# Routing moved into the experts' stage: early loads of the first weights, bf16 products for prefix sums and token lists, products of constants in TensorE's holes

## The chip, the cores and the metric

The kernel runs on one core of one Trainium2 chip. The metric is the device time of one execution, in microseconds. Three runs of the kernel before took 1526.89, 1527.82 and 1534.71 us, a median of 1527.82.

## What is computed

The program is one decoder layer over 1024 tokens of width 1024 in float32: an input projection, two groups of attention heads, an output projection, then a mixture of experts, then a gated per-layer embedding and a last normalisation. The change touches the head of the mixture of experts:

```
grp_logits = u @ w_group + b_group;  g_star = argmax(grp_logits)
in_prob = softmax(the 4 expert logits of g_star);  top_v, top_i = top_k(in_prob, 2)
w = grp_prob[g_star] * top_v / sum(top_v);  expert_id = g_star * 4 + top_i
for e in range(16):
    hid = silu(u @ w_gate_e[e]) * (u @ w_up_e[e])
    y += combine[e] * (hid @ w_down_e[e])
```

Each token goes to 2 of 16 experts. The kernel doesn't compute all 16 for every token. It sorts the 2048 (token, expert) pairs by expert into tiles of 128 rows, an expert's rows starting on a new tile, and computes tile by tile.

## The kernel before

The program is a row of stages. Each stage is a scope with its own semaphores, and a scope ends with a barrier of all engines, the clearing of its semaphores and a second barrier (`Scope.__exit__`, line 165). Within a stage every engine has a program of its own, written out by hand in the order in which it runs, and the engines meet at semaphores. The stages here are `stage_mix`, which ends with the routing logits in `lg`, then `stage_route`, then `stage_moe`, then `stage_finish`.

`stage_route` (scope `rte`) is one chain of small VectorE steps (L1676 to L1759), in which every step waits for the one before it. The maxima and the choices give `pick` (which expert for each of a token's two places) and `both` (their sum). Two float32 products on TensorE follow: `ps_r` (L1771), with a strictly triangular matrix, counts the earlier tokens of a block of 128 that chose the same expert, and `ps_t` (L1772), with a matrix of ones, gives each block's count. Eight additions over the blocks (L1707) give the prefix sums `off`. From the totals come the number of tiles of each expert, `cend` and `cbeg`, then `where` and the place `slot` of each pair. Then the list is turned round, from slot to token: `is_tile` (tile one-hot times token number) and `is_row` (row one-hot, 128x2048) are made on VectorE, and 16 float32 products sum them in `ps_s` (L1776). VectorE meanwhile makes the tile plan (`texp`, `last`, `tnew`, `tord`) and at last copies the list to `stok` (L1759).

`stage_moe` loops over the tiles. GpSimd copies a column of `stok` to `idx` (L1919) and gathers 128 rows of u with an indirect DMA into `xg` (L1921). TensorE turns them (L2106). ScalarE and VectorE split the result into a high and a low part (`xT_hi` L1964, `xT_lo` L2051). The sync engine (SP) loads an expert's weights in 8 chunks of gate and up (16 transfers at L1863) and 4 chunks of down (L1870). ScalarE and VectorE split each chunk as well (`g_hi` L1940, `g_lo` L2028). TensorE then does three products for each of 8 chunks and 2 matrices, 48 in all (`gate_up`, L138 to L140), turns the hidden values (L2124) and does 24 products for `down`. Each engine begins by reading `last` into a register (L1851). A chunk of the next expert's weights is loaded once both parts of the chunk before it are split. That wait stands in SP's program, so the chunks follow one another in order.

In `stage_moe` before the change, SP's program begins with the reads of `last` and of `texp` and then the 16 transfers for the first expert; ScalarE's begins with `x_part(0)`, then eight `split_g`; VectorE's with a memset of zeros, then `x_part(0)` and eight `split_g`.

Of the kernel before, what the change touches and what calls it, by code (L numbers as in the profile page):

```python
# [27 lines left out]
F32 = mybir.dt.float32  # L28
F32R = mybir.dt.float32r
BF16 = mybir.dt.bfloat16  # L30
I32 = mybir.dt.int32
# [1585 lines left out]
def stage_route(nc, K, T):  # L1617


    with Scope(nc, "rte") as sc:  # L1620
        def sb(name, *shape):
            return sc.sb(name, [P, *shape])

        gmax, gsum, gp, pm = (sb(n, NT) for n in ("gmax", "gsum", "gp", "pm"))
        dlt, pri, ohg, il, oh1, oh2, il2 = (sb(n, NT, 4) for n in ("dlt", "pri", "ohg", "il", "oh1", "oh2", "il2"))
        m1, m2, e2, v1 = (sb(n, NT) for n in ("m1", "m2", "e2", "v1"))
        prod = sb("prod", NT, NG, EPG)
        pick = [sb(f"pick{k}", NT, NG, EPG) for k in range(2)]
        both = sb("both", NT * NE)
        off = sb("off", NT + 1, NE)  # L1630
        tot = sb("tot", NT, NE)
        where = sb("where", NT, NE)
        cnt_i = sc.sb("cnt_i", [P, NE], I32)
        ntl, cend, cbeg, ones = (sb(n, NE) for n in ("ntl", "cend", "cbeg", "ones"))
        tile_ge = sb("tile_ge", 32, NE)
        tile_e = sb("tile_e", 32)
        tile_new = sb("tile_new", 32)
        tile_ord = sb("tile_ord", 32)
        n_last = sb("n_last", 1)
        slot_f = sb("slot_f", 2, NT)  # L1640
        row_f = sb("row_f", 2, NT)
        in_tile = sb("in_tile", 2, NT)
        slot_i = sc.sb("slot_i", [P, 2, NT], I32)
        is_row = sb("is_row", 2 * NT, P)
        is_tile = sb("is_tile", 2 * NT, SLOTS // P)
        ps_r = sc.ps("ps_r", [P, 512])
        ps_t = sc.ps("ps_t", [P, 512])
        ps_s = sc.ps("ps_s", [P, 512])
        own_dve, expd, want_exp, ranked, both_made, slots_made, named = (
            sc.sem(n) for n in ("own_dve", "expd", "want_exp", "ranked", "both_made", "slots_made", "named"))  # L1650
        c = K["c"]
        lg = K["lg"]
        with sc.block() as block:
            @block.vector
            def _(dve):
                own = Tally(own_dve)

                def step(ins):
                    own.inc(ins)
                    own.wait(dve)  # L1660

                V = nc.vector

                def wide(x, n=4):

                    return x[:].unsqueeze(2).to_broadcast((P, NT, n))

                def first_max(x, top, out):

                    step(V.tensor_tensor(pri[:], x, wide(top), ALU.is_equal))  # L1670
                    step(V.tensor_tensor(pri[:], pri[:], c[:, K_PRI:K_PRI + 4].unsqueeze(1).to_broadcast((P, NT, 4)),
                                         ALU.mult))
                    step(V.tensor_reduce(pm[:], pri[:], X, ALU.max))
                    step(V.tensor_tensor(out[:], pri[:], wide(pm), ALU.is_equal))

                step(V.memset(ones[:], 1.0))  # L1676
                step(V.tensor_reduce(gmax[:], lg[:, :, 0:NG], X, ALU.max))
                V.tensor_tensor(dlt[:], lg[:, :, 0:NG], wide(gmax), ALU.subtract).then_inc(want_exp, 1)
                first_max(lg[:, :, 0:NG], gmax, ohg)
                step(V.tensor_tensor(prod[:], lg[:, :, NG:].rearrange("p t (g j) -> p t g j", g=NG),  # L1680
                                     ohg[:].unsqueeze(3).to_broadcast((P, NT, NG, EPG)), ALU.mult))
                step(V.tensor_reduce(il[:], prod[:].rearrange("p t g j -> p t j g"), X, ALU.add))
                step(V.tensor_reduce(m1[:], il[:], X, ALU.max))
                first_max(il[:], m1, oh1)
                step(V.scalar_tensor_tensor(il2[:], oh1[:], NEG, il[:], ALU.mult, ALU.add))
                step(V.tensor_reduce(m2[:], il2[:], X, ALU.max))
                first_max(il2[:], m2, oh2)
                V.tensor_tensor(e2[:], m2[:], m1[:], ALU.subtract).then_inc(want_exp, 1)
                for k, oh in enumerate((oh1, oh2)):
                    step(V.tensor_tensor(pick[k][:], ohg[:].unsqueeze(3).to_broadcast((P, NT, NG, EPG)),  # L1690
                                         oh[:].unsqueeze(2).to_broadcast((P, NT, NG, EPG)), ALU.mult))
                V.tensor_tensor(both[:], pick[0][:].rearrange("p t g j -> p (t g j)"),
                                pick[1][:].rearrange("p t g j -> p (t g j)"), ALU.add).then_inc(both_made, 1)

                dve.wait_ge(expd, 2)
# [10 lines left out]
                for t in range(NT):  # L1706
                    step(V.tensor_tensor(off[:, t + 1, :], off[:, t, :], tot[:, t, :], ALU.add))  # L1707
# [761 lines left out]
```

## Time and profile before

| | us |
|---|---|
| median of three runs | 1527.82 |
| the profiled execution's own time | 1527.78 |
| its span | 1525.8 |
| TensorE busy in the span | 1370.0 (90%) |
| VectorE busy | 759.3 (50%) |
| ScalarE busy | 628.8 (41%) |
| GpSimd busy | 166.6 (11%) |

The span runs from the first to the last instruction, and the execution's own time is 2.0 us longer. All positions below are in us from the start of the span. The last logits are copied at 898.04, routing's own chain lasts from 900.60 to 925.27, and the products of the first tile begin at 941.23. The granted TensorE clock is given as a share of full speed: 1.00 is 2.4 GHz and 0.50 is 1.2 GHz.

### The profile page before, as it was taken

Reading aid. Unit: us, or ns where it says so; the run is one execution under the profiler, and the core shown is the slowest. Engines: PE = TensorE matmul, PEld = TensorE weight load, DVE = VectorE, ACT = ScalarE, POOL = GpSimd, SP = SyncE. Lnnn points to the kernel's source line nnn. Section 1 sums busy time; section 2 is a strip of 40 time slices with the busy share of each in tenths; the row PEclk is TensorE's granted clock in tenths of the full one; section 3 lists DMA queues with packets and bytes.
Section 4 is the critical chain, followed back from the end, with each engine's and each line's share of the span. In section 5 each row is a group of like instructions: output and inputs, shape, how many; then the busy total and the mean of one; then the engine's idle time right before and its main releaser. Section 6 shows DMA issues by size and latency. Waiting matters only on the chain. (4 is left out here: it accounts for less than half of the span.)

```text
span 1525.8 us, 24075 instructions
## 1 busy us (share of the span) xinstructions
PE 1370.0 (90%) x7956; PEld 1157.9 (76%) x7957; DVE 759.3 (50%) x1225; ACT 628.8 (41%) x932; POOL 166.6 (11%) x164
## 2 busy tenths in 40 slices
PE   5899999959999999999789955999999999928996
PEld 4788879949989988888678844777777787716774
DVE  4734013344544444433353344678655767846562
ACT  5312121023333334454442212567645666743442
POOL 2100000041111122322000000000100000011000
PEclk9999999969999999999889966999999999968998
DMA  7333311051100111443132206799976979784411
GB/s 249 96 89 110 117 60 52 3 125 26 26 22 22 36 43 43 126 112 71 39 117 97 110 28 237 274 324 382 353 247 234 351 291 350 275 313 138 135 61 42
DMA packets 107556, 222.23 MB, mean 146 GB/s; under 512 B 14717, under 2 KB 41389, under 8 KB 107478
## 3 DMA queue, kind: packets, MB, share of 16 engines
q1 hardware_dynamic: 95462, 178.87, 35.7%
q0 software_dynamic: 8608, 30.51, 5.7%
q10 hardware_dynamic: 3408, 11.80, 2.1%
q8 instruction: 50, 0.82, 0.2%
q14 instruction: 28, 0.23, 0.0%
HBM read 176.56 MB, written 36.24 MB: 139 GB/s over the span
## 5 line engine op out<-in xcount | busy, mean ns | idle before, releaser
L1253 ACT ACTIVATE att_prob<-att_ps_s 128x512 f32<-128x512 f32 (+1 forms) x240 | 134.6, 561 | 246.5 <-PE att_ps_s L1180 201.6
L1302 DVE TENSOR_REDUCE att_mx<-att_ps_m 128x1 f32<-128x512 f32 (+3 forms) x256 | 132.8, 561 | 134.5 <-PE att_ps_m L1127 122.8
L2028 DVE TENSOR_TENSOR exp_g_lo<-exp_g_raw,exp_g_hi 128x1024 fp32r<-128x1024 f32 x128 | 148.1, 1220 | 43.3 <-ACT exp_g_hi L1940 43.3
L138 PE MATMUL moe_ps_g<-exp_g_hi,moe_xT_hi 128*128 128x512 f32 x336 | 137.7, 410 | 16.8 <-DVE exp_g_lo L2028 16.8
L1940 ACT ACTIVATE exp_g_hi<-exp_g_raw 128x1024 fp32r<-128x1024 f32 x128 | 124.8, 1047 | 40.7 <-PE moe_ps_g L140 25.5
L1198 PE MATMUL att_ps_o<-tok_vsw,att_prob 128*128 128x65 f32 x1056 | 140.1, 274 | 0.0
L139 PE MATMUL moe_ps_g<-exp_g_lo,moe_xT_hi 128*128 128x512 f32 x336 | 133.9, 399 | 0.0
L140 PE MATMUL moe_ps_g<-exp_g_hi,moe_xT_lo 128*128 128x512 f32 x336 | 133.9, 398 | 0.0
L1198 PEld LDWEIGHTS att_ps_o<-tok_vsw,att_prob 128*128 128x128 f32 x1056 | 131.2, 192 | 2.6 <-ACT att_prob L1253 0.5
L138 PE MATMUL prj_ps_w<-prj_hT_hi,prj_w_hi 128*128 128x512 f32 x256 | 102.3, 399 | 5.6 <-ACT prj_w_hi L425 2.4
L140 PE MATMUL prj_ps_w<-prj_hT_hi,prj_w_lo 128*128 128x512 f32 x256 | 101.3, 396 | 0.0
L139 PE MATMUL prj_ps_w<-prj_hT_lo,prj_w_hi 128*128 128x512 f32 x256 | 101.3, 396 | 0.0
L138 PEld LDWEIGHTS moe_ps_g<-exp_g_hi,moe_xT_hi 128*128 128x128 f32 x336 | 64.0, 191 | 37.5 <-DVE exp_g_lo L2028 20.2
L2033 DVE TENSOR_TENSOR exp_d_lo<-exp_d_raw,exp_d_hi 128x1024 fp32r<-128x1024 f32 x64 | 74.0, 1220 | 21.8 <-ACT exp_d_hi L1946 21.8
L138 PE MATMUL moe_ps_y<-exp_d_hi,moe_hT_hi 128*128 128x512 f32 x168 | 68.9, 410 | 10.8 <-DVE exp_d_lo L2033 10.8
L1198 PE MATMUL att_ps_o<-tok_vb,att_prob 128*128 128x65 f32 x576 | 75.9, 273 | 0.0
L140 PEld LDWEIGHTS moe_ps_g<-exp_g_hi,moe_xT_lo 128*128 128x128 f32 x336 | 63.8, 190 | 15.6
L139 PEld LDWEIGHTS moe_ps_g<-exp_g_lo,moe_xT_hi 128*128 128x128 f32 x336 | 64.2, 191 | 13.8
L1198 PEld LDWEIGHTS att_ps_o<-tok_vb,att_prob 128*128 128x128 f32 x576 | 72.1, 192 | 1.9 <-ACT att_prob L1253 0.2
L1919 POOL COPY moe_idx<-all_stok 128x1 uint32 (+1 forms) x22 | 10.2, 463 | 551.3 <-PE moe_ps_x L2106 339.5
L1946 ACT ACTIVATE exp_d_hi<-exp_d_raw 128x1024 fp32r<-128x1024 f32 x64 | 62.3, 1045 | 19.1 <-issue 19.1
L433 ACT ACTIVATE att_w_out<-prj_ps_w 128x512 f32<-128x512 f32 x28 | 16.7, 598 | 124.3 <-PE prj_ps_w L140 124.3
(357 smaller groups left out, 2950.2 us busy)
## 6 DMA issues: line engine op xcount, KB each, us to landing
exp_g_raw<-in_w_gate_e SPq DMA_DIRECT2D x128, 256.0 KB, 4.7
exp_g_raw<-in_w_up_e SPq DMA_DIRECT2D x128, 256.0 KB, 5.4
exp_d_raw<-in_w_down_e SPq DMA_DIRECT2D x64, 512.0 KB
y_rows<-moe_y ACTq DMA_DIRECT2D x21, 512.0 KB, 6.1
prj_w_raw<-in_w_in SPq DMA_DIRECT2D x16, 512.0 KB, 4.0
att_q_raw<-feat SPq DMA_DIRECT2D x32, 256.0 KB, 4.9
feat<-att_w_out POOLq DMA_DIRECT2D x14, 512.0 KB, 2.9
att_k_raw<-feat SPq DMA_DIRECT2D x24, 256.0 KB, 6.0
```

The source lines that it names most:

```text
L138: nc.tensor.matmul(out, a_hi, b_hi, start=first, stop=False)
L139: nc.tensor.matmul(out, a_hi, b_lo, start=False, stop=False)
L140: return nc.tensor.matmul(out, a_lo, b_hi, start=False, stop=last)
L433: nc.scalar.activation(feat[:, s, h * 512:(h + 1) * 512], ps_w[:, h, :], ACT.Copy, scale=scale).then_inc(evac, 1)
L1198: last = nc.tensor.matmul(ps_o[:, u % 2, (q % 4) * HV:(q % 4 + 1) * HV], prob[:, b % PT, at + (q - qa) * P:at + (q - qa + 1) * P], value(k ...
L1253: nc.scalar.activation(prob[:, b % PT, 0:w], ps_s[:, b % ST, 0:w], ACT.Exp, scale=-1.0).then_inc(expd, 1)
L1302: last = nc.vector.tensor_reduce(mx[i % 2][:, col, q:q + 1], p[:, at:at + (kb - ka) * P], X, ALU.min)
L1919: nc.gpsimd.tensor_copy(idx[:], K["stok"][:, bass.ds(i, 1)]).then_inc(idx_set, 1)
L1940: nc.scalar.activation(g_hi[:, ch % GR], g_raw[:, ch], ACT.Copy).then_inc(s_ghi, 1)
L1946: nc.scalar.activation(d_hi[:, ch % DR], d_raw[:, ch], ACT.Copy).then_inc(s_dhi, 1)
L2028: nc.vector.tensor_tensor(g_lo[:, ch % GR], g_raw[:, ch], g_hi[:, ch % GR].bitcast(F32), ALU.subtract).then_inc(s_glo, 1)
L2033: nc.vector.tensor_tensor(d_lo[:, ch % DR], d_raw[:, ch], d_hi[:, ch % DR].bitcast(F32), ALU.subtract).then_inc(s_dlo, 1)
```

## The change

`stage_route` is gone as a stage. Its steps become the head of the engines' programs in `stage_moe`, without the barriers in between. Its tiles lie in the memory of the buffer `h`, which is filled much later, so they show as `exp_h`. Within the steps:

- The triangular matrix and the matrix of ones are cast to bf16 on GpSimd (`below`), and `both`, `is_row` and `is_tile` are bf16. The eight additions are replaced by eight bf16 products that add each block's counts to all later blocks and to a total in one PSUM tile.
- The first expert is named as soon as the totals are known (`e0`), and SP loads its 16 chunks behind that (`first_named`). The rest of the plan is signalled at the end (`planned`), and each engine reads `last` later.
- The token list is summed as two numbers (row in the block, block), each small enough for bf16. They are put together by one VectorE step, which signals `tokens_made` to GpSimd.
- ScalarE splits four chunks and VectorE two before they take the first x tile.
- TensorE runs 10, 16 and 20 products of constants (`spin`) before the counts, before the lists and before the first x tile. Their output is overwritten.

```diff
+def spin(nc, out, K, n):
+    for _ in range(n):
+        nc.tensor.matmul(out, K["c"][:, K_ID:K_ID + P].bitcast(BF16)[:, 0:P], K["c"][:, 0:2 * P].bitcast(BF16),
+                         start=True, stop=True)
...
             @block.sync
-                end = last_used(sp)
-                e0 = sp.value_load(K["texp"][0:1, 0:1], min_val=0, max_val=NE - 1)
-                load_g(e0)
+                sp.wait_ge(first_named, 1)
+                e0 = sp.value_load(K["e0"][0:1, 0:1], min_val=0, max_val=NE - 1)
+                load_g(e0)
+                sp.wait_ge(planned, 1)
+                end = last_used(sp)
...
             @block.gpsimd
-                end = last_used(pool)
+                nc.gpsimd.tensor_copy(below, c[:, K_LT:K_LT + 2 * P]).then_inc(ones_made, 1)
...
+                pool.wait_ge(tokens_made, 1)
                 gather(0)
+                pool.wait_ge(planned, 1)
+                end = last_used(pool)
...
             @block.scalar
-                end = last_used(act)
-                x_part(0)
-                for ch in range(GC):
-                    split_g(0, 0, ch, False)
+                for ch in range(EARLY):
+                    split_g(0, 0, ch, False)
+                x_part(0)
+                for ch in range(EARLY, GC):
+                    split_g(0, 0, ch, False)
+                act.wait_ge(planned, 1)
+                end = last_used(act)
...
             @block.vector
+                dve.wait_ge(ranked, 1)
+                step(V.tensor_scalar(ntl, ps_r[:, NT * NE:(NT + 1) * NE], float(P - 1), None, ALU.add))
...
+                step(V.tensor_scalar(none, cend, 0.5, None, ALU.is_lt))
+                step(V.tensor_reduce(e0_f[:, 0:1], none, X, ALU.add))
+                V.tensor_copy(K["e0"][:], e0_f[:, 0:1]).then_inc(first_named, 1)
...
+                step(V.scalar_tensor_tensor(where, cbeg.unsqueeze(1).to_broadcast((P, NT, NE)), float(P),
+                                            ps_r[:, 0:NT * NE].rearrange("p (t e) -> p t e", t=NT), ALU.mult, ALU.add))
...
+                step(V.tensor_scalar(is_tile[:, :, 0:32], hit.rearrange("p k t n -> p (k t) n"), c[:, K_TOK:K_TOK + 1], None,
+                                     ALU.mult))
...
+                V.scalar_tensor_tensor(K["stok"][:], found[:, 32:32 + SLOTS // P], float(P), found[:, 0:SLOTS // P],
+                                       ALU.mult, ALU.add).then_inc(tokens_made, 1)
...
             @block.tensor
-                end = last_used(pe)
+                spin(nc, ps_g[:, 0, :], K, 10)
+                pe.wait_ge(ones_made, 1)
+                pe.wait_ge(both_made, 1)
+                nc.tensor.matmul(ps_r[:, 0:NT * NE], below[:, 0:P], both, start=True, stop=False, skip_group_check=True)
+                for t in range(NT):
+                    n = NT - t
+                    last = nc.tensor.matmul(ps_r[:, (t + 1) * NE:(NT + 1) * NE], below[:, P:2 * P],
+                                            both[:, t * NE:(t + 1) * NE].unsqueeze(1).to_broadcast((P, n, NE)),
+                                            start=False, stop=t == NT - 1, skip_group_check=True)
+                last.then_inc(ranked, 1)
+                spin(nc, ps_g[:, 0, :], K, 16)
+                pe.wait_ge(slots_made, 1)
+                for n in range(2 * NT):
+                    last = nc.tensor.matmul(ps_s[:, 0:64], is_row[:, n, :], is_tile[:, n, :], start=n == 0,
+                                            stop=n == 2 * NT - 1)
+                last.then_inc(named, 1)
+                spin(nc, ps_g[:, 0, :], K, 20)
                 turn_x(0, True)
                 gate_up(0, True)
+                pe.wait_ge(planned, 1)
+                end = last_used(pe)
```

Three places show how rows move. On TensorE, between the end of the mixing stage and the first x tile, the difference of the two orders is this (L1620 is a product of constants, `exp_h` holds routing's tiles, L2106 turns the first x tile):

```order
-L1771 MATMUL rte_ps_r<-rte_both,all_c 128x128
-L1772 MATMUL rte_ps_t<-rte_both,all_c 128x128
-L1776 MATMUL rte_ps_s<-rte_is_tile,rte_is_row 128x32 x16
-L1653 UNCONDITIONAL_BRANCH
 L2095 UNCONDITIONAL_BRANCH
-L1851 TENSOR_LOAD all_last
-L1851 ISA x2
+L1620 MATMUL moe_ps_g<-all_c 128x512 x10
+L2143 MATMUL moe_ps_y<-exp_h 128x128
...
+L1620 MATMUL moe_ps_g<-all_c 128x512 x16
+L2153 MATMUL moe_ps_h<-exp_h 128x64 x16
+L1620 MATMUL moe_ps_g<-all_c 128x512 x20
```

One branch and the read of `last` are gone ahead of the first x tile, and 46 products of constants are new. On VectorE, before, from the token list to the first hidden tile:

```order
L1759 CAST all_stok<-rte_ps_s 128x32
L1653 UNCONDITIONAL_BRANCH
L2024 UNCONDITIONAL_BRANCH
L2066 MEMSET moe_zeros 128x256
L1851 TENSOR_LOAD all_last
L1851 ISA x2
L2051 TENSOR_TENSOR moe_xT_lo<-moe_ps_x,moe_xT_hi 128x512 x2
L2028 TENSOR_TENSOR exp_g_lo<-exp_g_raw,exp_g_hi 128x1024 x8
L2058 TENSOR_TENSOR moe_hid<-moe_act_g,moe_ps_g 128x512
```

And the same place on VectorE now, where the list (L2049) is followed by the rest of the plan up to `tord` (L2061):

```order
L2048 COPY exp_h<-moe_ps_h 128x64
L2049 SCALAR_TENSOR_TENSOR all_stok<-exp_h 128x32
...
L2061 CAST all_tord<-exp_h 128x32
L2062 MEMSET moe_zeros 128x256
L1923 TENSOR_TENSOR exp_g_lo<-exp_g_raw,exp_g_hi 128x1024 x2
L1946 TENSOR_TENSOR moe_xT_lo<-moe_ps_x,moe_xT_hi 128x512 x2
L1923 TENSOR_TENSOR exp_g_lo<-exp_g_raw,exp_g_hi 128x1024 x6
L1734 TENSOR_LOAD all_last
L1734 ISA x2
L1953 TENSOR_TENSOR moe_hid<-moe_act_g,moe_ps_g 128x512
```

The list is now made ahead of the plan, two of the eight weight splits stand ahead of the x tile's, and the stage's branches between them are gone.

## Rows read from the trace of the kernel before

**Rows 1.** Stretches: length, busy us (instructions) by engine, clock, DMA share, GB/s

```profile
926.00:936.00 10.00, 0.00 (x0) 0.00 (x0) 0.27 (x1) 0.00 (x0) 1.22 (x2) 0.50 0.65 217
1100.00:1300.00 200.00, 195.05 (x901) 156.86 (x900) 127.42 (x131) 118.13 (x140) 14.90 (x22) 1.00 0.81 291
```

**Rows 2.** Timeline, routing's first part: start, duration, engine, line, operation, [idle before]

```profile
898.04 0.33 DVE L1549 COPY all_lg<-mix_ps_l 128x160 f32<-128x160 f32 x1 [6.89 <-PE mix_ps_l L1600]
...
900.60 0.07 DVE L1676 MEMSET rte_ones<- 128x16 f32 x1 [2.23 <-PEq L165]
...
905.86 0.29 DVE L1692 TENSOR_TENSOR rte_both<-rte_pick 128x128 f32<-128x128 f32 x1
...
907.54 0.29 DVE L1704 COPY rte_tot<-rte_ps_t 128x128 f32<-128x128 f32 x1 [0.21 <-PE rte_ps_t L1772]
```

**Rows 3.** Timeline, VectorE from the prefix sums to the row one-hot

```profile
908.00 1.63 DVE L1707 TENSOR_TENSOR rte_off<-rte_off,rte_tot 128x16 f32<-128x16 f32 x8
909.67 0.17 DVE L1709 TENSOR_SCALAR rte_ntl<-rte_off 128x16 f32<-128x16 f32 x1
...
911.27 0.29 DVE L1718 SCALAR_TENSOR_TENSOR rte_where<-rte_cbeg,rte_where 128x128 f32<-128x128 f32 x1
...
915.58 2.29 DVE L1737 TENSOR_TENSOR rte_is_row<-all_c,rte_row_f 128x2048 f32<-128x2048 f32 x1
```

**Rows 4.** Timeline, the products of the token list and their copy

```profile
917.93 7.04 PE L1776 MATMUL rte_ps_s<-rte_is_tile,rte_is_row 128*128 128x32 f32 x32 [10.50 <-DVE rte_is_row L1737]
...
925.08 0.19 DVE L1759 CAST all_stok<-rte_ps_s 128x32 uint32<-128x32 f32 x1 [3.59 <-PE rte_ps_s L1776]
```

**Rows 5.** Timeline, from the list to the first tile's products

```profile
927.36 0.18 POOL L1919 COPY moe_idx<-all_stok 128x1 uint32<-128x1 uint32 x1 [211.81 <-issue]
928.09 0.36 SPq L1863 DMA_DIRECT2D exp_g_raw<-in_w_gate_e  x1
928.43 1.04 POOL L1921 DMA_INDIRECT moe_xg<-u_rows,moe_idx  x1 [0.89 <-POOL moe_idx L1919]
...
936.27 1.97 PE L2106 MATMUL moe_ps_x<-all_c,moe_xg 128*128 128x128 f32 x8 [11.31 <-DMA moe_xg<-u_rows,moe_idx]
...
937.42 0.39 SPq L1863 DMA_DIRECT2D exp_g_raw<-in_w_up_e  x1
...
939.85 9.18 DVE L2028 TENSOR_TENSOR exp_g_lo<-exp_g_raw,exp_g_hi 128x1024 fp32r<-128x1024 f32 x8 [0.25 <-ACT exp_g_hi L1940]
...
941.23 0.77 PE L138 MATMUL moe_ps_g<-exp_g_hi,moe_xT_hi 128*128 128x512 f32 x1 [2.98 <-DVE exp_g_lo L2028]
```

**Rows 6.** Timeline, TensorE: end of the first tile's 48 products, begin and end of another tile's

```profile
954.41 1.04 PE L2106 MATMUL moe_ps_x<-all_c,moe_xg 128*128 128x128 f32 x8
...
978.94 0.48 PE L138 MATMUL moe_ps_g<-exp_g_hi,moe_xT_hi 128*128 128x512 f32 x1
...
990.21 1.03 PE L2106 MATMUL moe_ps_x<-all_c,moe_xg 128*128 128x128 f32 x8
```

**Rows 7.** Stretches of the first tile's products, columns as in rows 1

```profile
942.00:945.00 3.00, 3.00 (x8) 2.32 (x8) 3.00 (x4) 3.00 (x4) 0.00 (x0) 0.50 1.04 395
947.00:954.00 7.00, 7.00 (x32) 5.63 (x31) 2.03 (x2) 0.75 (x1) 0.00 (x0) 1.00 1.05 387
```

**Rows 8.** The gathers of x: all 22, then the first alone

```profile
DMA to landing us min/median/max: 4.1/7.1/8.0
...
DMA to landing us min/median/max: 7.8/7.8/7.8
```

**Rows 9.** bf16 products (timeline); groups by form: busy, mean ns, idle before

```profile
401.06 0.39 PE L1127 MATMUL att_ps_m<-tok_maskb,tok_identb 128*128 128x128 bf16 x4
...
L558 DVE TENSOR_SCALAR att_sin<-att_sin,all_c 128x1024 f32<-128x1024 f32 x1 | 0.8, 755 | 1.2 <-ACT att_cos L463 1.2
...
L1029 POOL CAST att_w_two<-all_c 64x1024 fp32r<-64x1024 f32 x2 | 2.1, 1037 | 0.1
...
L1919 POOL COPY moe_idx<-all_stok 128x1 uint32 x21 | 10.0, 477 | 339.5 <-PE moe_ps_x L2106 339.5
```

More of the change, by code:

```diff
@@ L1827, in stage_moe, with small @@
         last_hi = sc.sem("last_hi")
+        (own_dve, expd, want_exp, ones_made, both_made, ranked, slots_made, named, first_named, planned, tokens_made) = (
+            sc.sem(n) for n in ("own_dve", "expd", "want_exp", "ones_made", "both_made", "ranked", "slots_made", "named",
+                                "first_named", "planned", "tokens_made"))
+        words = K["h"][:].rearrange("p a n -> p (a n)")
+        taken = 0
+        def small(*shape, dt=F32):
+            nonlocal taken
+            n = int(np.prod(shape)) // (2 if dt == BF16 else 1)
+            at, taken = taken, taken + n
+            v = words[:, at:taken]
+            if dt != F32:
+                v = v.bitcast(dt)
+            names = "abc"[:len(shape)]
+            return v if len(shape) == 1 else v.rearrange(f"p ({' '.join(names)}) -> p {' '.join(names)}",
+                                                         **dict(zip(names[1:], shape[1:])))
+        gmax, gsum, gp, pm, m1, m2, e2, v1 = (small(NT) for _ in range(8))
+        dlt, pri, ohg, il, oh1, oh2, il2 = (small(NT, 4) for _ in range(7))
+        prod = small(NT, NG, EPG)
+        pick = [small(NT, NG, EPG) for _ in range(2)]
+        where = small(NT, NE)
+        ntl, cend, cbeg, ones, none = (small(NE) for _ in range(5))
+        cnt_i = small(NE, dt=I32)
+        tile_ge = small(32, NE)
+        tile_e, tile_new, tile_ord = (small(32) for _ in range(3))
+        e0_f, n_last = small(2), small(2)
+        slot_f, row_f, in_tile = (small(2, NT) for _ in range(3))
+        slot_i = small(2, NT, dt=I32)
+        hit = small(2, NT, 32)
+        found = small(64)
+        both = small(NT * NE, dt=BF16)
+        below = small(2 * P, dt=BF16)
+        is_row = small(2 * NT, P, dt=BF16)
+        is_tile = small(2 * NT, 64, dt=BF16)
+        assert taken <= HB * D
+        lg = K["lg"]
+        ps_r, ps_s = ps_y[:, 0, :], ps_h[:]
         wl_d = a["w_ple_gate"].rearrange("l (k p) n -> (l k) p n", p=P)
@@ new lines, in _ @@
+                step(V.tensor_copy(tile_ge[:, :, 0], tile_new))
+                step(V.memset(tile_ge[:, :, 1], 1.0))
+                step(V.tensor_tensor_scan(tile_ord, tile_ge[:, :, 1], tile_ge[:, :, 0], 0.0, ALU.mult, ALU.add))
+                V.tensor_copy(K["tord"][:], tile_ord).then_inc(planned, 1)
+                nc.vector.memset(zeros[:], 0.0).then_inc(zero_made, 1)
+                for ch in range(2):
+                    split_g(0, ch)
+                x_part(0)
+                for ch in range(2, GC):
+                    split_g(0, ch)
@@ L2067, in _ @@
+                dve.wait_ge(planned, 1)
                 end = last_used(dve)
-                x_part(0)
-                for ch in range(GC):
-                    split_g(0, ch)
                 hidden(0)
@@ L2438, in build @@
             stage_mix(nc, a, K, T)
-        stage_route(nc, K, T)
         with Scope(nc, "exp") as exp:
```

218 lines of the change are left out of this document (78 added, 140 removed).

## The prediction

> **What bounds the kernel now.** I read the stretches first. While the experts run, TensorE is busy 195 of 200 us [rows 1], so a microsecond taken from before their first product should come off the end of the span as well, as long as the later tiles keep their distances. Then I read the timeline between the last logits at 898.04 [rows 2] and the first expert product at 941.23 [rows 5]. In these 43.2 us TensorE does little but wait. The chain is: barrier (2.2 us idle ahead of 900.60), VectorE's small steps up to the row one-hot at 915.58 [rows 2, 3], 16 list products (7.0 us) and the copy at 925.08 [rows 4], barrier to 927.36, gather issued at 928.43, x there at 936.27, x split, first weights split, product at 941.23 [rows 5]. Each is late only by the one before it. The weights' transfers begin at 928.09 and their last issue is at 937.42, beside the gather. In the ten microseconds 926 to 936 no compute engine but GpSimd and one memset works, and the clock stands at 0.50. The first 48 products take 13.18 us (941.23 to 954.41), those of a later tile 11.27 (978.94 to 990.21) [rows 5, 6], because the first ones find the clock at 0.50 and get 1.00 only on the way [rows 7].
>
> **The change part by part**, in positions of the trace of before.
>
> *Up to the counts.* The choices' steps are the same ones. The memset of ones moves from their front behind them, which evens out. `both` ends at about 906.1 as before. VectorE has six small steps for the weights of the combination to do and was only 0.21 us early at 907.54 [rows 2], so it is nearly ready whatever the counts cost. Four bf16 products fit in 0.39 us, pipeline latency included [rows 9], so nine take at most 0.9 us at full clock and 1.8 at half: counts at 907.1 to 908.0. I take 907.5, a gain of nothing (-0.1 to +0.5). The ten products of constants before them are 512 columns each like the experts', 11.27/48 = 0.235 us at full clock and at most twice that at half, 4.7 us. They start at 900.6 and are over by 905.3, before `both`.
>
> *Counts to row one-hot.* Gone: the copy of totals, the memset and the eight additions, 909.67 - 907.54 = 2.13 us [rows 2, 3]. A small step costs 1.67/8 = 0.21 us with its wait. New: compare, reduce and cast for `e0`, the cast without a wait, 0.5 us. Two steps for `where` become one, -0.33. The cast to `slot` moves behind, -0.21. The token number's product stays as two steps for the block, and a scalar product over 512 elements is added: 0.755 us for 1024 [rows 9] gives 0.38, with its wait 0.44. Sum: -2.13 + 0.5 - 0.33 - 0.21 + 0.44 = -1.73. `is_row` starts at 913.8 instead of 915.58 and its 2.35 us (915.58 to 917.93) stay, since its inputs are float32 as before and only the output is bf16. The lists start at 916.15.
>
> *The lists.* 32 float32 passes pairwise took 7.04 us at clock 0.50, 0.22 each [rows 4]. Now there are 16 bf16 products. At half clock each is at most a float32 record's half, 0.11, so 1.8 us, at full clock 0.9 to 1.6 by the 0.1 above. I take 2.0 with the end's latency: 918.15. VectorE's slot, tile comparison and reduction end at about 917.7, and do not hold it up. Two more steps (copy from PSUM, combination) 0.45: `tokens_made` at 918.6, against 925.27.
>
> *No barrier.* From there GpSimd's first copy stood 2.09 us later, at 927.36. A wait on a semaphore costs 0.2: 918.8. The gather is issued 1.07 later as before, at 919.9. That is 8.5 us early.
>
> *The weights.* `e0` comes after five small steps from the counts (four of 0.21 and a scan, 1.07) and the 0.5 above: 909.1. SP reads one register (two cost it 1.4 between 926.7 and 928.1, so 0.7) and starts at 909.9 instead of 928.09. 16 issues need 937.42 + 0.39 - 928.09 = 9.7 us, to 919.6, just before the gather. ScalarE then splits four chunks and VectorE two while x is on its way. VectorE has first to finish the plan, 2.4 us (the same steps as before), the zeros and two splits of 1.2, until 924. That is before x has come.
>
> *x arrives.* The first gather took 7.8 us in competition with the weights; the 22 lie between 4.1 and 8.0 [rows 8]. Now the weights' 4.2 MB, started 18 us earlier, are nearly all in when the gather starts. I take 5.8, between the two cases: 925.7 (bounds 924.0 and 927.9). TensorE's 20 products of constants run from 918.2 and take 4.7 us at full clock and at most 9.4 at half, ending 922.9 to 927.6. So they may hold x up by a microsecond: turning starts at 926.2, 10.1 us early.
>
> The Trainium skill, "Trainium Kernel Development and Optimization", Key Constraints, speaks against this place: transfers from the queues of SP, ScalarE and GpSimd all run on the same 16 DMA engines and interleave, so an early gather still shares them with the tail of the early weights. By that rule alone the landing stays near 7.8 us and the time is 2 us longer, still inside my range. The first gather's 7.8 against the least of 4.1 agrees with it.
>
> *x to first product.* Before: 936.27 to 941.23, of which x's own split ends at 939.60 (0.25 ahead of 939.85) and the rest is the first weights' split [rows 5]. That second part goes: 3.33 us remain, or 2.6 at full clock, where turning takes 1.04 [rows 6] instead of 1.97. I take 2.9: first product at 929.1, 12.1 us early. What is late next is x itself, no longer the weights. VectorE makes chunk 3's low part 1.2 us after x's, and TensorE asks for it 2.8 us after.
>
> *Clock.* The first 48 products cost 13.18 us when they start at half clock and 11.27 when at full. With 20 products of constants right before, I take 12.0, a gain of 1.2 (0 to 1.9).
>
> The Trainium skill, "TensorE: Matmul & The Clock Gate", Part 1, says that the array stands at half rate by default and that sustained work releases it. The fall to 0.50 before 941 and the return in rows 7 agree. By that rule the full 1.9 is had if constants run right up to x, none if the hole behind them is long.
>
> *What is unchanged.* The reads of `last` move behind work with slack: VectorE and ScalarE wait for TensorE at the first tile's end. From 954.41 on the order is the same and shifts as a whole.
>
> **Sum.** 12.1 + 1.2 = 13.3 us against the execution's own 1527.78, which is the median within 0.04: 1514.5. With the slowest landing, 3.33 and a cold start: 927.9 + 3.3 = 931.2, gain 10.0, less 0.5 for the counts, 1518.3. With the fastest landing, 2.6 and a warm start: 924.0 + 2.6 = 926.6, gain 14.6 + 1.9 = 16.5, so 1511.3.
>
> **Rivals.**
>
> *A. Late x, cold clock.* The gather is as slow as before or slower because the weights, not finished, share its engines, and the holes after the constants let the clock fall. For it: 7.8 us in the one case like it. Against: the issues are over when the gather starts. Gain 8 to 11, 1518.5.
>
> *B. The early steps don't run as written.* GpSimd's cast of two matrices to bf16, or VectorE's steps beside it, are slow. A cast of 64x1024 takes 1.04 us, so 256 columns 0.3 [rows 9], ready 5 us before it is needed. "GPSIMD Engine Reference" (the Trainium skill), its table's row on SBUF interfaces, says that GpSimd shares them with VectorE and that VectorE instructions with two SBUF inputs contend. The index copy agrees: 0.477 us among the weights' subtractions [rows 9], 0.18 alone [rows 5]. That would make 0.3 of the new gather's copy at most. It is slower than before only if the cast takes over 5.5 + 13.3 = 19 us from 900.6; every microsecond over 5.5 costs one, and a cast of 25 us would give 1534. Nothing in the rows comes near that.
>
> *C. The gain is given back.* The second expert's loads, or the tiles' later waits, don't move with the first product, because DMA at 395 GB/s [rows 7] is the bound there. Against: over the long stretch the DMA share is 0.81 and TensorE's 195 of 200 [rows 1], and loads start earlier than the products do. Gain under 7.6, say 1522.
>
> **Chances.** Forecast 0.65, A 0.25, C (and part of B) 0.08, B slower than before 0.02. The predicted time is the forecast's. The range 1510.5 to 1519.5 holds the sum's two ends and A, and leaves out C and B. A measurement of this kernel can tell 0.5%, 7.6 us, from no change: faster 0.92, same 0.06, slower 0.02.
>
> **What would show it.** In the new profile: first SP transfer of the experts 18 us ahead of before, list products under 2 us, GpSimd's first copy at about 918.8, 20 us or less after the first routing step, TensorE's first x tile at about 926, first product 2.6 to 3.3 us later, with a clock of 1.00 or soon. From the first tile's end to the span's end the distance should be 571.4 us as before (1525.8 - 954.4). I am wrong if that distance grows, if x lands later than 928, or if TensorE still works at the constants when x is there for more than 2 us.

## The result, and the profile after

The changed kernel takes 1518.27 us, the median of 7 runs (1516.01 to 1521.95). The kernel before, with runs beside these, has a median of 1529.42 of 7 (1526.89 to 1534.71). The ratio is 0.993 with a 95% interval of 0.9913 to 0.9947, so the change is 11 us faster (8 to 13). The forecast was 1514.5 in a range of 1510.5 to 1519.5, so the time came out inside the range and 3.8 us above the number. The profiled execution took 1516.79 us with a span of 1515.1, against 1527.78 and 1525.8 before.

The stages ahead of the change run a little earlier or later in each execution. So positions are counted here from the start of the copy of the last logits, which lies at 898.04 before [rows 2] and at 898.54 after. I write +30.5 for 30.5 us behind it. First the timeline of VectorE after (start, duration, engine, line, operation, idle before), answering to rows 2, 3 and 4:

```profile
898.54 0.32 DVE L1549 COPY all_lg<-mix_ps_l 128x160 f32<-128x160 f32 x1 [6.89 <-PE mix_ps_l L1600]
901.15 0.19 DVE L1980 TENSOR_REDUCE exp_h<-all_lg 128x8 f32<-128x32 f32 x1 [2.29 <-PEq L165]
...
907.76 0.17 DVE L2004 TENSOR_TENSOR all_cw<-all_cw,exp_h 128x8 f32<-128x8 f32 x1
907.97 0.17 DVE L2008 TENSOR_SCALAR exp_h<-moe_ps_y 128x16 f32<-128x16 f32 x1
...
914.32 2.29 DVE L2038 TENSOR_TENSOR exp_h<-all_c,exp_h 128x2048 bf16<-128x2048 f32 x1
...
917.46 0.69 DVE L2046 TENSOR_REDUCE exp_h<-exp_h 128x32 f32<-128x512 f32 x1
918.18 0.22 DVE L2048 COPY exp_h<-moe_ps_h 128x64 f32<-128x64 f32 x1
```

From behind 901.15 up to the list no row has idle time before it: in routing VectorE never waits for a product any more, neither for the counts (907.97, where it waited 0.21 before) nor for the lists (918.18, where it waited 3.59). Next TensorE after, with the products of constants (L1620) between the useful ones:

```profile
901.06 4.24 PE L1620 MATMUL moe_ps_g<-all_c 128*128 128x512 bf16 x10 [2.56 <-PEq L165]
906.75 0.22 PE L2143 MATMUL moe_ps_y<-exp_h 128*128 128x128 bf16 x1 [1.45 <-DVE exp_h L1995]
906.81 0.43 PE L2146 MATMUL moe_ps_y<-exp_h 128*128 128x128 bf16 x8
907.10 3.61 PE L1620 MATMUL moe_ps_g<-all_c 128*128 128x512 bf16 x16
916.67 1.03 PE L2153 MATMUL moe_ps_h<-exp_h 128*128 128x64 bf16 x16 [5.96 <-DVE exp_h L2038]
917.51 6.71 PE L1620 MATMUL moe_ps_g<-all_c 128*128 128x512 bf16 x20
926.35 1.10 PE L2106 MATMUL moe_ps_x<-all_c,moe_xg 128*128 128x128 f32 x8 [2.12 <-DMA moe_xg<-u_rows,moe_idx]
929.02 0.80 PE L138 MATMUL moe_ps_g<-exp_g_hi,moe_xT_hi 128*128 128x512 f32 x1 [1.57 <-DVE moe_xT_lo L1946]
...
941.78 1.04 PE L2106 MATMUL moe_ps_x<-all_c,moe_xg 128*128 128x128 f32 x8
```

The lists take 1.03 us instead of 7.04 [rows 4]. The first expert product now waits for x's low part (L1946), not for the weights' low part as in rows 5. It comes at +30.48, before at +43.19. GpSimd and SP after, answering to rows 5, and the first gather's landing, to rows 8:

```profile
918.70 0.18 POOL L1804 COPY moe_idx<-all_stok 128x1 uint32<-128x1 uint32 x1 [17.26 <-DVE all_stok L2049]
919.77 1.04 POOL L1806 DMA_INDIRECT moe_xg<-u_rows,moe_idx  x1 [0.90 <-POOL moe_idx L1804]
...
910.63 0.36 SPq L1746 DMA_DIRECT2D exp_g_raw<-in_w_gate_e  x1
...
DMA to landing us min/median/max: 6.5/6.5/6.5
```

And stretches of the kernel after (length, busy us of TensorE, its weight loads, VectorE, ScalarE, GpSimd, then clock, DMA share, GB/s), for rows 7:

```profile
907.00:911.00 4.00, 3.71 (x24) 1.55 (x21) 3.42 (x18) 0.00 (x0) 0.00 (x0) 1.00 0.01 2
911.00:916.00 5.00, 0.00 (x0) 0.00 (x0) 4.69 (x10) 1.06 (x1) 0.00 (x0) 0.92 0.79 279
916.00:922.00 6.00, 5.33 (x27) 2.45 (x28) 5.42 (x19) 3.17 (x3) 1.22 (x2) 0.50 1.05 390
922.00:928.00 6.00, 3.33 (x18) 1.64 (x16) 1.67 (x3) 0.95 (x2) 0.18 (x1) 1.00 0.83 288
929.00:932.00 3.00, 2.98 (x7) 2.43 (x8) 3.00 (x3) 2.98 (x5) 0.70 (x1) 0.50 0.52 143
```

The constants raise the clock to 1.00 twice, and it is lost again twice: during the hole of 5.96 us ahead of the lists, and at x. There it outlives the hole of 2.12 us, since turning still takes 1.10 us (1.97 at half clock, e2), and is gone behind the next one of 1.57 us. The first 48 products begin at 0.50, as before.

### The profile page after: what moved, and what is told of

Read it like the earlier page. It is cut to its first block and busy times, and to the rows that moved or that the text cites. A ratio compares the mean times of both kernels' runs of the same rounds, so it can differ in the third digit from the quotient of the medians.

```text
span 1515.1 us, 24106 instructions
## 1 busy us (share of the span) xinstructions
PE 1379.2 (91%) x7991; PEld 1158.4 (76%) x7992; DVE 758.6 (50%) x1219; ACT 628.9 (42%) x932; POOL 167.0 (11%) x165
## 3 DMA queue, kind: packets, MB, share of 16 engines
q1 hardware_dynamic: 95462, 178.87, 36.2%
## 5 line engine op out<-in xcount | busy, mean ns | idle before, releaser
L138 PE MATMUL moe_ps_g<-exp_g_hi,moe_xT_hi 128*128 128x512 f32 x336 | 138.2, 411 | 15.0 <-DVE exp_g_lo L1923 13.3
L1928 DVE TENSOR_TENSOR exp_d_lo<-exp_d_raw,exp_d_hi 128x1024 fp32r<-128x1024 f32 x64 | 74.1, 1220 | 22.2 <-ACT exp_d_hi L1834 22.2
L139 PE MATMUL moe_ps_y<-exp_d_lo,moe_hT_hi 128*128 128x512 f32 x168 | 67.3, 401 | 0.0
```

The costliest lines, as they stand in the source:

```text
L138: nc.tensor.matmul(out, a_hi, b_hi, start=first, stop=False)
L139: nc.tensor.matmul(out, a_hi, b_lo, start=False, stop=False)
L1928: nc.vector.tensor_tensor(d_lo[:, ch % DR], d_raw[:, ch], d_hi[:, ch % DR].bitcast(F32), ALU.subtract).then_inc(s_dlo, 1)
```

## The experiments

Theory 1: the gain is a sum of independent parts, the shorter chain to the list, the missing barrier, and the first weights being ready before x. The constants buy only the faster turning. Rival 2: the constants' clock carries the gain. Rival 3: the early load of the weights does. The table gives each kernel's positions in its trace, in us; "gather to landing" is the time from GpSimd's instruction to x's arrival, and "its 48 products" reach from the first product to the turning of the second x tile. Each line is one execution, so the two lines of the same kernel, after and e10, show what chance can do: 0.6 us in the gather and at the first product, 1.2 us in the 48 products.

| kernel | list | gather to landing | x turned | first product | its 48 products | third x tile |
|---|---|---|---|---|---|---|
| before | +27.0 | 7.8 | +38.2 | +43.2 | 13.2 | +74.1 |
| after | +19.9 | 6.5 | +27.8 | +30.5 | 12.8 | +62.1 |
| e1 stage kept, products changed | +21.6 | 7.6 | +32.6 | +37.5 | 12.8 | +69.4 |
| e2 no constants | +19.9 | 6.2 | +27.5 | +30.9 | 12.8 | +61.0 |
| e3 late load | +19.9 | 4.5 | +25.9 | +36.2 | 13.2 | +66.9 |
| e4 x first | +19.9 | 6.6 | +27.9 | +32.1 | 13.6 | +63.2 |
| e5 late load, x first | +19.9 | 4.3 | +25.7 | +30.9 | 12.9 | +62.6 |
| e6 float32 products | +27.6 | 4.4 | +33.3 | +36.0 | 12.7 | +67.5 |
| e7 holes filled | +19.9 | 6.6 | +27.8 | +30.5 | 11.3 | +57.9 |
| e8 gather alone | +19.9 | 4.6 | +25.9 | +28.6 | 11.3 | +57.4 |
| e9 e7 and e8 | +19.9 | 4.5 | +25.8 | +28.5 | 12.2 | +56.7 |
| e10 after again | +19.9 | 7.1 | +28.4 | +31.1 | 14.0 | +62.7 |
| e11 two chunks held | +19.9 | 5.2 | +26.5 | +29.2 | 11.3 | +56.5 |

**e1, the products alone**, in a stage of their own:

```diff
 # stage_route of before
-                dve.wait_ge(ranked, 2)
...
-                for t in range(NT):
-                    step(V.tensor_tensor(off[:, t + 1, :], off[:, t, :], tot[:, t, :], ALU.add))
+                dve.wait_ge(ranked, 1)
+                step(V.tensor_scalar(ntl[:], ps_r[:, NT * NE:(NT + 1) * NE], float(P - 1), None, ALU.add))
```

> Positions are counted from the start of the copy of the last logits (before: list copied at +27.0, first product at +43.2; after: list at +19.9, first product at +30.5). This kernel is the one before with only the products changed: bf16 prefix sums in PSUM and bf16 token lists, in their own stage with its barriers, weights behind it, no constants, x ahead of the splits. Theory 1 (the gain is three independent parts: shorter routing chain 7 us, barrier 2 us, first weights and gather 3 to 4 us): list at +20.4, first product at +36.6, 6.7 us faster than before, some 1522.7. Rival (the bf16 products only pay with the clock that the constants hold): list at +23 or later, at most 4 us faster.

Measured: 1526.09 us, ratio 0.9979 (0.9964 to 0.9995). The list comes at +21.6, the first product at +37.5, 5.7 us earlier than before. The medians differ by 4.1 us with an interval of 0.8 to 5.5, so the time alone would fit the rival too; the positions decide, since the list comes before the rival's +23. The gain is a microsecond short of mine, because in this kernel the plan still stands ahead of the list, so its copy waits for VectorE's own steps and not for TensorE:

```profile
917.70 2.29 DVE L1730 TENSOR_TENSOR rte_is_row<-all_c,rte_row_f 128x2048 bf16<-128x2048 f32 x1
920.04 1.03 PE L1782 MATMUL rte_ps_s<-rte_is_tile,rte_is_row 128*128 128x64 bf16 x16 [8.56 <-DVE rte_is_row L1730]
923.84 0.23 DVE L1753 COPY rte_found<-rte_ps_s 128x64 f32<-128x64 f32 x1
926.38 0.18 POOL L1925 COPY moe_idx<-all_stok 128x1 uint32<-128x1 uint32 x1 [20.98 <-issue]
```

The list products are over at 921.07, and VectorE takes them up at 923.84. From the list (924.10) to GpSimd's copy the barrier costs 2.28 us; in the merged kernels that distance is 0.26.

**e2, no constants**:

```diff
-                spin(nc, ps_g[:, 0, :], K, 10)
...
-                spin(nc, ps_g[:, 0, :], K, 16)
...
-                spin(nc, ps_g[:, 0, :], K, 20)
```

> The kernel after without its 46 products of constants. Theory 1: the clock had fallen to 0.50 at the list products of after anyway and they took 1.03 us, so only the turning of the first x tile gets slower (1.97 instead of 1.10 us) and the counts by 0.2: first product at +31.3, time 1 us above the kernel after. Rival 2 (the constants carry the first products' clock): first 48 products 13.2 us or more, list later by 1 us, in all 3 us or more above after.

Measured: 1517.37 us, ratio to before 0.9913 (0.9883 to 0.9943), no difference from the kernel after that can be told. Rival 2 falls.

```profile
911.36 0.68 PE L2145 MATMUL moe_ps_y<-exp_h 128*128 128x128 bf16 x8
921.22 1.03 PE L2151 MATMUL moe_ps_h<-exp_h 128*128 128x64 bf16 x16 [9.17 <-DVE exp_h L2038]
930.60 1.97 PE L2106 MATMUL moe_ps_x<-all_c,moe_xg 128*128 128x128 f32 x8 [8.35 <-DMA moe_xg<-u_rows,moe_idx]
933.98 0.79 PE L138 MATMUL moe_ps_g<-exp_g_hi,moe_xT_hi 128*128 128x512 f32 x1 [1.41 <-DVE moe_xT_lo L1946]
```

The lists take the same 1.03 us with and without constants, the counts 0.25 more, and turning 0.87 more, of which 0.7 lies on the path (3.38 from turning to first product, 2.67 in after). That is all the constants give as they are placed. At the first product 0.4 us are left of that, since the gather landed 0.3 us sooner here. The time was 1 us below after, not above, which is inside the interval.

**e5, late load and x first**, two halves of the change undone:

```diff
+                sp.wait_ge(planned, 1)
                 e0 = sp.value_load(K["e0"][0:1, 0:1], min_val=0, max_val=NE - 1)
                 load_g(e0)
-                sp.wait_ge(planned, 1)
...
+                x_part(0)
                 for ch in range(2):
                     split_g(0, ch)
-                x_part(0)
```

> The kernel after with the first weights' transfers only behind the whole plan, and x ahead of all weight splits, as before. Theory 1: the gather has the DMA engines to itself for 2 us and lands in 4.5 to 7 us instead of 6.4, the first chunk lands 3.4 us after its issue at +23.1, so the first product comes at +30 to +32.6, 0 to 2 us above the kernel after: the early load itself is worth little. Rival 3 (the early load is a main part): first product at +33.5 or later, time 3 us or more above after.

Measured: 1519.51 us, ratio 0.9925 (0.9899 to 0.9951), no difference from the kernel after that can be told. Rival 3 falls. The first product is at +30.9, 0.4 us behind after, but 0.2 ahead of the same changed kernel in e10. In e5 and in e10:

```profile
936.73 0.77 PE L138 MATMUL moe_ps_g<-exp_g_hi,moe_xT_hi 128*128 128x512 f32 x1 [4.15 <-DVE exp_g_lo L1921]
...
929.58 0.79 PE L138 MATMUL moe_ps_g<-exp_g_hi,moe_xT_hi 128*128 128x512 f32 x1 [1.57 <-DVE moe_xT_lo L1946]
```

The logits' copies are at 905.84 and 898.49, so the two stand at +30.89 and +31.09. The early load of all eight chunks, with its order of splits, is therefore worth nothing that these traces can tell from zero. It costs what it brings: x comes 2.1 us earlier without it (2.7 against e10).

**e3, late load, splits still first**, and **e4, early load, x first**, each one half of e5's edit:

> The kernel after with the first weights' transfers behind the whole plan; ScalarE and VectorE still split four and two chunks ahead of x. Before: first product at +43.2 from the last logits' copy, after +30.5, late load with x first +30.9. Theory 1: x lands after 4.3 us as in the late load with x first, at +25.6, but ScalarE must first split chunk 3, which lands about 4 us after chunk 0 at +26.8, so x's high part waits to +32 and the first product comes at +33.5 to +35: the order of the splits pays only together with the early load. Rival (the order makes no difference): +31.

> The kernel after (early load) with x ahead of all eight splits. Theory 1: x lands after 6.4 us, at +27.7, is split by +30.4, the first weights' split (1.05 + 1.22, minus overlap) comes after: first product at +32.0, 1.5 us later than after. Rival: +30.5 as after, since ScalarE's split of chunk 0 overlaps VectorE's work on x.

Measured, one run each: e3 1520.38, first product at +36.2; e4 1518.14, first product at +32.1. Both the way theory 1 had it; e4 hits its number, e3 is 1.2 us beyond the range that I gave. ScalarE in e3:

```profile
927.63 1.06 ACT L1828 ACTIVATE exp_g_hi<-exp_g_raw 128x1024 fp32r<-128x1024 f32 x1 [21.24 <-DMA exp_g_raw<-in_w_up_e]
929.41 1.06 ACT L1828 ACTIVATE exp_g_hi<-exp_g_raw 128x1024 fp32r<-128x1024 f32 x1 [0.72 <-DMA exp_g_raw<-in_w_up_e]
...
932.20 1.06 ACT L1828 ACTIVATE exp_g_hi<-exp_g_raw 128x1024 fp32r<-128x1024 f32 x1 [0.29 <-DMA exp_g_raw<-in_w_up_e]
933.17 1.06 ACT L1852 ACTIVATE moe_xT_hi<-moe_ps_x 128x512 fp32r<-128x512 f32 x2
```

x was turned at 924.77 and its high part waited until 933.17 behind four chunks. So splits first and early load belong together: the order saves 1.6 us with the early load (+32.1 to +30.5) and loses 5.3 without it (+30.9 to +36.2).

**e6, float32 products** (same products, no cast):

```diff
-        both = small(NT * NE, dt=BF16)
+        both = small(NT * NE)
...
+        is_row = spare[:, 0:2 * NT * P].rearrange("p (a n) -> p a n", n=P)
```

> The kernel after with float32 instead of bf16 in the counts' and lists' products (same products, no cast on GpSimd, which then does nothing there). Theory 1: 32 records of 0.22 us instead of 16 of 0.06 in the lists and 0.5 us more for the counts put the list at +26.3 and the first product at +36.8, time 6 us above after. Rival (the passes are hidden beside VectorE's plan, which takes 1.6 us): under 5 us above after.

Measured: 1521.46 us, ratio 0.995 (0.9932 to 0.9967). The list comes at +27.6, 7.7 us later than after, the first product only 5.5 later, since the weights are all in when the gather starts and it lands in 4.4 us. bf16 is thus worth 7.7 us at the list and 5.5 at the first product, where I expected 6.3. The medians lie only 3.2 us apart, with overlapping intervals, so the time alone would fit the rival's "under 5 us"; the positions decide here as well. The rows of its TensorE show both costs, counts and lists, and the last one VectorE waiting for the lists:

```profile
910.54 3.44 PE L2148 MATMUL moe_ps_y<-exp_h,all_c 128*128 128x128 f32 x16
...
922.80 6.18 PE L2155 MATMUL moe_ps_h<-exp_d_raw 128*128 128x64 f32 x32 [3.82 <-DVE exp_d_raw L2040]
...
929.09 0.22 DVE L2050 COPY exp_h<-moe_ps_h 128x64 f32<-128x64 f32 x1 [4.82 <-PE moe_ps_h L2155]
```

The counts' nine products take 4.0 us instead of 0.5. That I had put at 0.5 more. They put the row one-hot off by 2.9 us, and the wait for the lists adds 4.8.

**e7, holes filled**:

```diff
-                spin(nc, ps_g[:, 0, :], K, 16)
+                spin(nc, ps_g[:, 0, :], K, 38)
...
-                spin(nc, ps_g[:, 0, :], K, 20)
+                spin(nc, ps_g[:, 0, :], K, 38)
                 turn_x(0, True)
+                spin(nc, ps_g[:, 0, :], K, 7)
...
+                spin(nc, ps_y[:, 0, :], K, 12)
                 gate_up(1)
```

> The kernel after with more products of constants: 38 instead of 16 before the lists, 38 instead of 20 before the first x tile, 7 between its turning and the first product, 12 before the second tile's products. Theory 1: with no hole over 1 us the granted clock stays at 1.00 from the counts on, the first 48 products take 11.3 instead of 12.8 us and the second tile's 11.3 instead of 14: 2 to 4 us below the kernel after, if the constants end before x at +27.8. Rival 2 (the clock falls by something else, such as the power of the whole chip, or the constants don't count): same as after or later.

Measured, one run: 1513.25 us, 5.0 below the median of after, more than the 2 to 4 that I expected. The clock is 1.00 in every stretch from the counts through the second tile:

```profile
918.00:929.00 11.00, 8.94 (x55) 4.09 (x54) 7.41 (x20) 3.17 (x3) 1.22 (x2) 1.00 0.94 347
929.00:943.00 14.00, 13.90 (x64) 10.60 (x65) 8.10 (x8) 6.16 (x7) 1.17 (x2) 1.00 0.87 298
```

The first product stands where it stood (+30.5), its 48 take 11.3 us, and the third x tile is turned at +57.9 instead of +62.1. So constants do pay, when they leave no long hole: 4.3 us here against after (3.2 against e2, which has none), while the 46 of the change give 0.7 us behind the turning of x and no time that can be told.

**e8, the gather alone**:

```diff
                     for ch in range(GC):
+                        if before is None and ch == EARLY:
+                            sp.wait_ge(x_in, 16)
```

> The kernel after, but SP issues only the first four weight chunks early and the other four once x has landed. Theory 1: the gather doesn't share the DMA engines and lands in 4.3 us instead of 6.5, x is turned at +25.7 and the first product comes at +28.4, 2 us earlier than after, and chunks 4 to 7 land before they are needed. Rival (the landing doesn't depend on the weights in flight): +30.5, or later because of the held-back chunks.

Measured, one run: 1514.19 us. Landing in 4.6 us, first product at +28.6, 1.9 us earlier than after, as expected. The constants now run right up to x:

```profile
925.45 2.68 PE L1620 MATMUL moe_ps_g<-all_c 128*128 128x512 bf16 x10
928.14 1.10 PE L2108 MATMUL moe_ps_x<-all_c,moe_xg 128*128 128x128 f32 x8
930.81 0.50 PE L138 MATMUL moe_ps_g<-exp_g_hi,moe_xT_hi 128*128 128x512 f32 x1 [1.57 <-DVE moe_xT_lo L1948]
```

In this execution the clock stayed at 1.00 and the 48 took 11.3 us. The same 20 constants had no hole behind them here, because x came 2 us earlier; one trace doesn't show that it is always so. The comparison with e5 says more about the early load than e5 alone: in both kernels the gather runs undisturbed and x is turned at +25.7 and +25.9, but the first product is 2.3 us earlier here. Four chunks loaded early and split before x are worth that; all eight lose it again at the gather.

**e9, both**, with 34, 27, 6 and 12 constants, beside **e10, the changed kernel again**:

> Both at once: the last four weight chunks held until x has landed, and 34, 27, 6 and 12 products of constants in the holes. Positions from the last logits' copy; third x tile turned in after at +62.1, filled +57.9, gather alone +57.4. Theory 1: the two gains add, since one shortens the wait and the other the products: first product at +28.4, its 48 in 11.3 us, third x tile turned at +55.7, and the time 6 us below the kernel after, 1512. Rival (an earlier x collides with the constants, or the held-back weights become the bound at full clock): +57 or later, 3 us or less below after.

> The changed kernel unchanged, beside the one above. All theories: first product at +30.5 again; the 48 products take between 11.3 and 13.2 us by where the clock returns, and the median lies 10 to 12 us below before.

Measured: e9 1513.39 us, ratio to before 0.9898 (0.9879 to 0.9917); e10 1519.21, 0.9934 (0.9919 to 0.995). e9 beats both kernels: the slowest of its 4 runs (1515.38) is below the fastest of e10's 6 (1516.35). Its third x tile comes at +56.7, a microsecond later than the sum of the gains and just ahead of the rival's +57. The held-back chunks became late, ScalarE waiting for the last one, and TensorE behind it inside the 48 products, which take 12.2 us at a clock of 1.00:

```profile
933.78 1.06 ACT L1830 ACTIVATE exp_g_hi<-exp_g_raw 128x1024 fp32r<-128x1024 f32 x1 [3.17 <-DMA exp_g_raw<-in_w_up_e]
...
936.15 0.50 PE L138 MATMUL moe_ps_g<-exp_g_hi,moe_xT_hi 128*128 128x512 f32 x1 [0.58 <-DVE exp_g_lo L1925]
```

e10's median lies 10.3 us below before, as expected. Its first product came at +31.1, not again at +30.5, because the gather took 7.1 us. Its 48 products took 14.0 us, longer than the 11.3 to 13.2 I had allowed: they began at 929.58, and the clock came back only between 935 and 936 (in after between 932 and 933).

**e11, two chunks held instead of four** (`ch == GC - 2`):

> Gather alone and filled holes together, with only the last two weight chunks held until x has landed instead of the last four (with four, chunk 7 landed late among the second expert's loads and the second matrix's last products waited 0.6 us). Theory 1: six chunks issued by +17.7 are in by +22, when the gather's rows begin to flow, so x still lands in 4.5 us and is turned at +25.8; the last chunk comes in time, the 48 products take 11.3 us and the third x tile is turned at +55.8, 0.8 us earlier than with four held. Time 6 to 7 us below the kernel after. Rival (six chunks in flight slow the gather as eight do): x turned at +27.5 or later, third x tile at +57.5.

Measured: 1513.62 us, ratio 0.9897 (0.9882 to 0.9913), not to be told from e9. The 48 products take 11.3 us again, but x lands in 5.2 us and is turned at +26.5, between my 4.5 and the rival's. One gain was changed for the other.

## Why the prediction was right, and which term was not

*Up to the counts.* Right: VectorE takes them at +9.43, predicted +9.46, and it did not wait.

*Counts to row one-hot.* Right. 914.32 - 898.54 = +15.78, predicted 913.8 - 898.04 = +15.8.

*Lists.* The product count was right and the price too high, 1.03 instead of 2.0 us. It is hidden anyway, since VectorE's tile comparison ends at 918.15 and the copy follows at once. The cover is thin, 0.45 us (the products end at 917.70): in e6 they stick out by 4.8.

*No barrier.* Right: 0.26 us from list to GpSimd's copy, and 2.28 with it (e1).

*The weights.* Right. The first transfer goes out at +12.1, predicted +11.9, and the 16 issues take 7.8 us (910.63 to 918.47) instead of 9.7.

*x arrives.* 6.5 us for the landing where I took 5.8, and 7.1 in e10. The choice between the bounds came out nearer to contention. Key Constraints of "Trainium Kernel Development and Optimization" (the Trainium skill) says that transfers issued from the queues of SP, ScalarE and GpSimd all run on the same 16 DMA engines and interleave. The traces agree: the gather takes 7.6 to 7.8 us with the weights issued at the same moment (before, e1), 6.2 to 7.1 with eight chunks just issued (after, e2, e4, e7, e10), 5.2 with six (e11), and 4.3 to 4.6 with four (e8, e9), with all eight already in (e6) or with the weights 2.2 us behind it (e3, e5). The half microsecond that I took for the constants holding x up did not come: they ended 2.12 us before it.

*x to first product.* 2.67 us where I took 2.9: TensorE turned at full clock in 1.10 us. The first product is at +30.48, predicted +31.1: the gather was issued 0.6 us earlier than predicted, from there to the turning it took 0.3 longer, and from the turning 0.2 less. What is late is x, as forecast: holding the weights back moved the product by 1.9 us (e8).

*Clock.* This is the mis-sized term. I took 12.0 us for the first 48 products, a gain of 1.2; they took 12.8, and in e10 14.0, which is no gain at all. In both the clock stood at 0.50 at the first product, after constants that ended 2.12 us (2.77 in e10) before x and a hole of 1.57 us behind the turning. Without any constants (e2) they took the same 12.8. e7 and e8 show the 11.3 us of the other end.

*What is unchanged.* Here one of my own signs of being wrong came true. I expected 571.4 us from the end of the first 48 products to the end of the span. It is 1515.1 - 941.78 = 573.3. The next tile shows 1.2 of these 1.9: from the second to the third x tile it is 18.88 us after (43.24 to 62.12), before 17.71, although from its turning to its first product it takes less (4.77 against 5.02). It ran at half clock for longer:

```profile
946.55 0.80 PE L138 MATMUL moe_ps_g<-exp_g_hi,moe_xT_hi 128*128 128x512 f32 x1 [2.53 <-DVE exp_g_lo L1923]
947.14 0.63 PE L139 MATMUL moe_ps_g<-exp_g_lo,moe_xT_hi 128*128 128x512 f32 x1
...
952.26 0.63 PE L139 MATMUL moe_ps_g<-exp_g_lo,moe_xT_hi 128*128 128x512 f32 x1
952.69 0.43 PE L140 MATMUL moe_ps_g<-exp_g_hi,moe_xT_lo 128*128 128x512 f32 x1
```

Slow products follow each other from 946.55 to 952.69. By the table the same section takes 17.4 to 19.0 us in the nine other traces with that hole, and 16.0 to 16.1 where it is filled (e7, e9, e11). The changed kernel's other trace, e10, has 17.6 there, and from the end of its 48 products to the end of its span it has 571.1 us, so neither the 1.2 nor the remaining 0.7 is a price of the change. The ten traces with that hole lie between 570.4 and 573.9 us, with before's 571.4 among them. What I lacked was this scatter of about 2 us to each side: against a single trace, "if that distance grows" was no fair test. Where the 0.7 us lie in the later stages was not followed up.

*The sum.* From the last logits to the end of the 48 products the gain is 56.37 - 43.24 = 13.1 us, against 13.3 forecast. The start at 898.54 instead of 898.04 and the 1.9 make it 10.7 in the span. The distance of the medians is 11.2. So the miss of 3.8 us (1518.27 against 1514.5) is 2.1 in the gain and 1.6 in the reference: over 7 runs before has 1529.42, not the 1527.82 that I started from.

*The rivals.* A (late x, cold clock) came half true: the clock was cold, the landing less slow. Its 1518.5 is the nearest number to the measured time, but that is luck: the first product came even before the forecast's, and 1.6 us of the distance are the reference. B did not happen: the cast took 0.40 us at 901.03, over 5 us before its use, and the gather's copy 0.18 us. C did not happen either: the distance behind the first tile grew by 1.9 us in this trace and shrank by 0.3 in e10's, and what was followed of it is the clock, not the DMA engines.

One reading under B was wrong. The index copy's 0.477 us is the mean of two durations and not what it takes among the weights' subtractions. Of 22 copies in before 14 took 0.18 us and 8 took 0.95 to 0.96. Those 8, and no others, begin within a subtraction of down's weights, which has both inputs in SBUF:

```profile
1029.38 1.22 DVE L2033 TENSOR_TENSOR exp_d_lo<-exp_d_raw,exp_d_hi 128x1024 fp32r<-128x1024 f32 x1
1029.68 0.96 POOL L1919 COPY moe_idx<-all_stok 128x1 uint32 x1 [16.87 <-PE moe_ps_x L2106]
```

The short ones start beside VectorE steps that read PSUM (`moe_hid`, `xT_lo`), or beside nothing. In after it is 14 and 8 again. So what such a step can add to a copy is 0.8 us, not the 0.3 of the prediction.

Of the 12.7 us at the first product, e1 gives 5.7 to the changed products. From e1 to e5 the merge brings 6.6: 1.7 by the list ahead of the plan, 2.0 by the barrier, 3.1 between GpSimd's copy and the turning, since the weights are now issued 2.2 us behind the gather and no longer 0.3 ahead of it, less 0.2 behind the turning. The early load with its order adds 0.4, which is inside the scatter, since it takes 2.1 back from the gather. So of theory 1's three parts two are shown. The third, the first weights ready before x, is not worth anything by itself as the change has it: a kernel that loads them late gets as far, through its faster gather. The constants' 0.4 at the first product is inside these numbers.

## What to carry to other kernels

When a small gather and a large load both precede the first product, ask which of them is awaited last and let that one go alone. Issuing all of the other early gave nothing that can be told from zero here, even with the consumer's order changed too; issuing half of it early and holding the rest back until x had landed gave 2.3 us at the first product (e8 against e5). Constants in TensorE's holes paid here only where they left no long hole on either side of the real work: 46 of them, with 5.96 us free ahead of the lists and 2.12 and 1.57 us around x, left the first products at half clock; 105 (e7), with at most 1.3 us free, took 3 to 4 us off the first two tiles, and with 89 and up to 2.1 us free (e9, e11) the clock stayed at 1.00 as well. A step moved in front of a wait needs its data early, or it blocks what stands behind it (e3, 5 us). And a single trace of one kernel moved by 0.6 us at the first product and by 1 to 2 us behind it, so a part worth less than that needs more than one.

## What was not expected of the hardware

The 16 bf16 list products took 1.03 us at a granted clock of 0.50 (after, e2) and 0.64 at 1.00 (e9, 915.19):

```profile
915.19 0.64 PE L2155 MATMUL moe_ps_h<-exp_h 128*128 128x64 bf16 x16 [2.09 <-DVE exp_h L2040]
```

At half clock that is 0.06 us for a product of 64 columns with its weights of 128 columns. The float32 form took 6.18 us for 32 records (e6, the first of them still at 1.00), six times as much for twice the records. The loading of the weights may be what sets this pace, which no run tests by itself. In before TensorE's weight loads (the second busy time of the row) have nearly no gap while the lists are summed:

```profile
918.00:925.00 7.00, 6.96 (x32) 6.83 (x32) 2.98 (x13) 0.00 (x0) 0.00 (x0) 0.50 0.00 0
```

The 32 float32 loads are busy for 6.9 us, the 16 bf16 loads of after for 0.9 us, at the same clock.

The same kernel's first 48 products took 12.8 us in one execution and 14.0 in another, with every step ahead of them within 0.7 us. Where the clock returned differed between these executions, and single traces differ by 1 to 2 us through it.
